# Feed-forward up projections in seven half-size products instead of eight

## The reference

```
y = rms_norm(h, mlp_norm_g[layer])
h = h + square(relu(y @ w_up[layer])) @ w_down[layer]      # w_up 1024 x 4096, w_down 4096 x 1024, f32
```

## Time and profile before

| | |
|---|---|
| runs | 2162.52, 2160.38, 2161.98 us; median 2161.98 |
| profiled execution | span 2157.4 us, its only time in the profile; 4.6 below the median of the runs |
| busy: PE, PEld, DVE, ACT, POOL | 2132.0, 1776.3, 1167.1, 892.1, 966.0 us |
| granted clock of TensorE | 0.997 in the mean |
| two feed-forward stages | from about 1153 to 1490 and 1795 to 2143 us |

### The profile page before, as it was taken

One profiled execution on the slowest core, in us unless ns is written; L12 is line 12 of the kernel. 1 busy time (PEld: TensorE's weight loads), 2 busy tenths in 40 slices (PEclk: granted clock), 3 DMA queues, 4 the chain that ended last, 5 costly groups with the idle time before them and its releaser, 6 DMA issues.

```text
span 2157.4 us, 29579 instructions
## 1 busy us (share of the span) xinstructions
PE 2132.0 (99%) x10318; PEld 1776.3 (82%) x10318; DVE 1167.1 (54%) x1715; ACT 892.1 (41%) x1321; POOL 966.0 (45%) x707
## 2 busy tenths in 40 slices
PE   9999999999999999999999999999999999999998
PEld 7888888778888888878888888888788887888886
DVE  7655556887777777787355222224565565222223
ACT  5433233555655555455534223224345444233223
POOL 4443535355444444316445445444443325444443
PEclk9999999999999999999999999999999999999999
DMA  6232222232222222223222222224212212222221
GB/s 225 87 103 83 97 83 78 89 137 98 79 78 78 84 91 78 104 82 117 98 78 98 98 96 85 98 97 130 98 63 75 79 59 79 98 97 97 97 97 59
DMA packets 38416, 202.09 MB, mean 94 GB/s; under 512 B 4395, under 2 KB 9643, under 8 KB 16076
## 3 DMA queue, kind: packets, MB, share of 16 engines
q1 hardware_dynamic: 29504, 191.46, 25.2%
q10 hardware_dynamic: 8844, 9.70, 1.5%
HBM read 195.90 MB, written 5.24 MB: 93 GB/s over the span
## 4 chain that ended last, share of the span: by engine, by line
PE 89%; DVE 6%; issue 2%; DVEq 2%; ACT 1%; POOL 0%; DMA 0%; POOLq 0%; SPq 0%; ACTq 0%
PE bank L450 15%; PE bank L451 15%; PE bank L456 15%; PE bank L437 12%; PE bank L438 12%; PE bank L439 12%; DVE SS L1799 1%; PE bank L970 1%; PE bank L490 1%; DVE X L2022 1%; PE bank L732 1%; PE bank L491 1%; PE bank L495 1%; DVE T L2019 1%; ACT WH L1126 1%
## 5 line engine op out<-in xcount | busy, mean ns | idle before, releaser
L368 POOL TENSOR_TENSOR WL<-RAW,WH 128x512 fp32r<-128x512 f32 x700 | 959.8, 1402 | 1162.6 <-ACT WH L1126 1162.6
L1126 ACT ACTIVATE WH<-RAW 128x2048 fp32r<-128x2048 f32 (+1 forms) x190 | 337.2, 1777 | 591.3 <-PE bank L439 288.1
L450 PE MATMUL bank<-HH,WH 128*128 128x512 f32 x968 | 382.7, 395 | 0.8 <-DVEq L2353 0.8
L451 PE MATMUL bank<-HL,WH 128*128 128x512 f32 x968 | 377.3, 390 | 0.0
L456 PE MATMUL bank<-HH,WL 128*128 128x512 f32 x968 | 241.5, 391 | 0.0
L450 PEld LDWEIGHTS bank<-HH,WH 128*128 128x128 f32 x968 | 181.8, 188 | 39.9 <-DVEq L2353 1.0
L456 PEld LDWEIGHTS bank<-HH,WL 128*128 128x128 f32 x968 | 181.6, 188 | 39.9 <-issue 2.4
L451 PEld LDWEIGHTS bank<-HL,WH 128*128 128x128 f32 x968 | 181.9, 188 | 37.7 <-issue 1.0
L2319 DVE TENSOR_TENSOR X<-X,bank 128x512 f32<-128x512 f32 x128 | 87.6, 686 | 193.7 <-PE bank L456 117.5
L2310 DVE SCALAR_TENSOR_TENSOR TG<-bank,RS 128x512 f32<-128x512 f32 x64 | 44.0, 688 | 206.9 <-PE bank L439 135.8
L437 PE MATMUL bank<-HH,WH 128*128 128x512 f32 x288 | 112.2, 390 | 0.7 <-DVE HL L1788 0.7
(11 more groups left out here) (440 smaller groups left out, 4364.7 us busy)
## 6 DMA issues: line engine op xcount, KB each, us to landing
RAW<-panels SPq DMA_DIRECT2D x174, 1024.0 KB, 4.8
X<-xin SPq DMA_DIRECT2D x4, 512.0 KB, 7.6
xsave<-X ACTq DMA_DIRECT2D x4, 512.0 KB, 2.8
X<-xsave ACTq DMA_DIRECT2D x1, 2048.0 KB, 13.7
TAB<-scratch ACTq DMA_DIRECT2D x16, 128.0 KB, 3.1
out<-ACC SPq DMA_DIRECT2D x8, 256.0 KB, 2.3
RAW<-panels SPq DMA_DIRECT2D x2, 512.0 KB, 6.6
T<-xtok SPq DMA_DIRECT2D x2, 512.0 KB, 12.7
```

The costliest lines, as they stand in the source:

```text
L368: gp.tensor_tensor(WL[:, s, cs], RAW[:, s, cs], WH[:, s, cs].bitcast(f32), ALU.subtract).then_inc(lo_ready, 1)
L450: nc.tensor.matmul(o, wh[:, columns[k - k0]], xh[:, k, :], start=first and k == k0, stop=False)
L451: nc.tensor.matmul(o, wh[:, columns[k - k0]], xl[:, k, :], start=False, stop=False)
L1126: return nc.scalar.activation(dst, src, ACT.Copy)
```

## The change

Chunk 0 stays as it was (PLAIN = 1). In chunks 1 to 7 an up panel of 256 hidden features is a 2x2 block product: the panel has four blocks (near and far 128 features, upper and lower 512 inputs) and the tokens four (upper and lower 512 inputs, first and last 256 tokens). Instead of eight block products of 12 matmuls (48 of 512 columns in all) it makes seven, of 12 matmuls with 256 columns each, in Winograd's form of Strassen's scheme: products 2 to 4 take sums of weight blocks (SUMS, split into EH and EL) and sums of token blocks (TOK, split into TOKH and TOKL), product 6 a weight block and a sum of tokens, product 7 a sum of weights that stands in the panel itself. The texts call the two halved panels of a chunk H0 and H1; the order on PE is H0, H1, D0, D1.

The sums of tokens are made once for each layer, in chunk 0, behind its hidden tiles: DVE norms all tokens (NORMED), makes four sums, ACT and DVE split sums and normed tokens. DVE makes the weight sums of each halved panel from RAW, writing the last over RAW's fourth block, ahead of ACT's split of that panel. Products 5 and 7 add onto the banks of products 1 and 4. DVE adds the products up from PSUM; ACT copies the first product and the sum of products 1 and 5 out of a bank that is used again. The relu and the square are one DVE operation here. The bias table's DMAs move behind the last hidden part. To make room, buffers share memory, and several semaphores of other stages are merged under one name each with shifted counts (`z_made`, `tanh_made`, `squared`, `mix_prepared`), which is not shown; nor are the parts that chunk 0 and the down panels keep.

```diff
+PLAIN = 1
+HALVES = CHUNKS - PLAIN
+PARTS_SPLIT = 2 + 2 * HALVES
...
+    TOKH = sb("TOKH", [128, 4, 4, 256], f32r, c)
...
+    with ExitStack() as c2:
+        TOK = sb("TOK", [128, 4, 4, 256], f32, c2)
+        NORMED = sb("NORMED", [128, KD, 512], f32, c2)
+    TOKL = sb("TOKL", [128, 4, 4, 256], f32r, c)
+    EH, EL = sb("EH", [128, 2, 3, 512], f32r, c), sb("EL", [128, 2, 3, 512], f32r, c)
...
+        def product(o, a, b, waits=None, onto=False):
+            (ah, al), (bh, bl) = a, b
+            for k in range(4):
+                cs = slice(128 * k, 128 * k + 128)
+                nc.tensor.matmul(o[:, 0:256], ah[:, cs], bh(k), start=k == 0 and not onto, stop=False, skip_group_check=onto)
+                nc.tensor.matmul(o[:, 0:256], ah[:, cs], bl(k), start=False, stop=False, skip_group_check=onto)
+            if waits is not None:
+                low_up_to(*waits)
+            for k in range(4):
+                cs = slice(128 * k, 128 * k + 128)
+                end = nc.tensor.matmul(o[:, 0:256], al[:, cs], bh(k), start=False, stop=k == 3, skip_group_check=onto)
+            return end
+        def halved_panel(i, u):
+            n, s = i * 4 + (n0 + 4 * PLAIN + u), i * 2 + (2 * HALVES * L + u)
+            w = panel(n, (n0 + u) % 2)
+            wh, wl = w[:2]
+            b0 = 4 - 4 * u
+            def block_of_w(j):
+                cs = slice(512 * j, 512 * j + 512)
+                return (wh[:, cs], wl[:, cs])
+            def sum_of_w(j):
+                return EH[:, u, j, :], EL[:, u, j, :]
+            def block_of_h(k0, t0):
+                return (lambda k: HH[:, k0 + k, t0:t0 + 256]), (lambda k: HL[:, k0 + k, t0:t0 + 256])
+            def sum_of_h(j):
+                return (lambda k: TOKH[:, j, k, :]), (lambda k: TOKL[:, j, k, :])
+            made = S["up_product"]
+            pe.wait_ge(S["up_parts_split"], PARTS_SPLIT * L + 2)
+            pe.wait_ge(hi_ready, n + 1)
+            o1 = bank(b0)
+            product(o1, block_of_w(0), block_of_h(0, 0), (w, 0)).then_inc(made, 1)
+            pe.wait_ge(S["up_parts_split"], i * 2 + (PARTS_SPLIT * L + 3 + u))
+            product(bank(b0 + 1), sum_of_w(1), sum_of_h(1)).then_inc(made, 1)
+            product(bank(b0 + 3), sum_of_w(2), sum_of_h(2)).then_inc(made, 1)
+            o3 = bank(b0 + 2)
+            product(o3, sum_of_w(0), sum_of_h(0)).then_inc(made, 1)
+            pe.wait_ge(S["up_copied"], i * 4 + (4 * HALVES * L + 2 * u + 1))
+            product(o1, block_of_w(1), block_of_h(4, 0), (w, 512), True).then_inc(made, 1)
+            product(bank(b0 + 1), block_of_w(2), sum_of_h(3), (w, 1024)).then_inc(made, 1)
+            pe.wait_ge(S["up_fifth_read"], s + 1)
+            product(o3, block_of_w(3), block_of_h(4, 256), (w, 1536), True).then_inc(panel_used, 1)
         first_panel(n0)
         if L == 0:
             sum_of_squares(name)
-        else:
-            other_panels(0, True)
-            first_panel(n0 + 4)
-        with pe.Fori(L, CHUNKS - 1) as c:
-            uses.loop(c, [2] * 4 + [1] * 4, first=L)
-            other_panels(c)
-            first_panel(c * 4 + (n0 + 4))
-        uses.end(CHUNKS - 1 - L)
-        other_panels(CHUNKS - 1)
+        other_panels(0, L == 1)
+        with pe.Fori(0, HALVES) as i:
+            uses.loop(i, [2, 3, 2, 2, 2, 3, 2, 2])
+            halved_panel(i, 0)
+            halved_panel(i, 1)
+            down_panels(i * 4 + (n0 + 4 * PLAIN + 2), i * 4 + (4 * CHUNKS * L + 4 * PLAIN))
+        uses.end(HALVES)
...
+        def high_tokens():
+            act.wait_ge(S["up_parts_f32"], PARTS_SPLIT * L + 2)
+            hi(TOKH[:, :, :, :], TOK[:, :, :, :]).then_inc(S["up_parts_hi"], 1)
+        def high_normed():
+            act.wait_ge(panel_used, n0 + 4 * PLAIN - 2)
+            hi(HH[:, 0:4, 0:256], NORMED[:, 0:4, 0:256])
+            hi(HH[:, 4:8, :], NORMED[:, 4:8, :]).then_inc(S["up_parts_hi"], 1)
+        def high_sums(i, u):
+            act.wait_ge(S["up_parts_f32"], i * 2 + (PARTS_SPLIT * L + 3 + u))
+            hi(EH[:, u, :, :], SUMS[:, :, :]).then_inc(S["up_parts_hi"], 1)
+        def high_of_chunk(i):
+            high_sums(i, 0)
+            split_in(i, 4, n0 + 4 * PLAIN)
+            high_sums(i, 1)
+            split_in(i, 4, n0 + 4 * PLAIN + 1)
+        def halved_chunk(i):
+            s = i * 2 + 2 * HALVES * L
+            for u in range(2):
+                b0 = 4 - 4 * u
+                act.wait_ge(S["up_product"], i * 12 + (12 * HALVES * L + 6 * u + 1))
+                hi(TG[:, u, 0:256], B[b0][:, 0:256]).then_inc(S["up_copied"], 1)
+                act.wait_ge(S["up_product"], i * 12 + (12 * HALVES * L + 6 * u + 5))
+                hi(T[:, 2 * u + 1, 0:256], B[b0][:, 0:256]).then_inc(free[b0], 1)
+                act.drain().then_inc(S["up_copied"], 1)
+                for f in range(2):
+                    if f == 1:
+                        split_in(i, 4, n0 + 4 * PLAIN + 2 + u)
+                    act.wait_ge(S["mlp_relu"], i * 4 + (4 * CHUNKS * L + 4 * PLAIN + 2 * u + f + 1))
+                    hi(HIDH[:, 2 * u + f, :], T[:, 2 * u + f, :]).then_inc(S["mlp_hid_hi"], 1)
+        plain_chunk(0)
+        high_tokens()
+        high_normed()
+        act.drain()
+        high_of_chunk(0)
+        with act.Fori(0, HALVES - 1) as i:
+            halved_chunk(i)
+            high_of_chunk(i + 1)
+        halved_chunk(HALVES - 1)
         if L == 0:
+            act.wait_ge(S["rows_stored"], 64)
+            for kind in range(4):
+                bias_table(kind)
             split_at(n0 + 4 * CHUNKS)
...
+        def normed():
+            for k in range(KD):
+                end = v.scalar_tensor_tensor(NORMED[:, k, :], X[:, k, :], gain(f"mlp{L}", k), RS[:, :], ALU.mult, ALU.mult)
+            end.then_inc(S["up_parts_f32"], 1)
+            ve.drain()
+        def sums_of_tokens():
+            b11, b12, b21, b22 = (NORMED[:, k:k + 4, t:t + 256] for k in (0, 4) for t in (0, 256))
+            v.tensor_tensor(TOK[:, 0], b12, b11, ALU.subtract)
+            v.tensor_tensor(TOK[:, 2], b22, b12, ALU.subtract)
+            ve.drain()
+            v.tensor_tensor(TOK[:, 1], b22, TOK[:, 0], ALU.subtract)
+            ve.drain()
+            v.tensor_tensor(TOK[:, 3], b21, TOK[:, 1], ALU.subtract)
+            ve.drain().then_inc(S["up_parts_f32"], 1)
+        def low_tokens():
+            ve.wait_ge(S["up_parts_hi"], PARTS_SPLIT * L + 1)
+            lo(TOKL[:, :, :, :], TOK[:, :, :, :], TOKH[:, :, :, :]).then_inc(S["up_parts_split"], 1)
+        def low_normed():
+            ve.wait_ge(S["up_parts_hi"], PARTS_SPLIT * L + 2)
+            lo(HL[:, 0:4, 0:256], NORMED[:, 0:4, 0:256], HH[:, 0:4, 0:256])
+            lo(HL[:, 4:8, :], NORMED[:, 4:8, :], HH[:, 4:8, :])
+            ve.drain().then_inc(S["up_parts_split"], 1)
+        def sums_of_w(i, u):
+            slot, first = (n0 + u) % 2, n0 + 4 * PLAIN + u
+            a11, a12, a22, a21 = (RAW[:, slot, 512 * j:512 * j + 512] for j in range(4))
+            ve.drain()
+            ve.wait_ge(raw_loaded[slot], i * 32 + (first // 2 * 16 + 16))
+            v.tensor_tensor(SUMS[:, 2], a11, a21, ALU.subtract)
+            v.tensor_tensor(SUMS[:, 0], a21, a22, ALU.add)
+            ve.drain()
+            v.tensor_tensor(SUMS[:, 1], a22, SUMS[:, 2], ALU.subtract)
+            ve.drain()
+            v.tensor_tensor(a21, a12, SUMS[:, 1], ALU.subtract)
+            ve.drain().then_inc(S["up_parts_f32"], 1)
+        def low_sums(i, u):
+            ve.wait_ge(S["up_parts_hi"], i * 2 + (PARTS_SPLIT * L + 3 + u))
+            lo(EL[:, u, :, :], SUMS[:, :, :], EH[:, u, :, :]).then_inc(S["up_parts_split"], 1)
+        def halved_up(i, u):
+            b0 = 4 - 4 * u
+            made, ahead = S["up_product"], 12 * HALVES * L + 6 * u
+            first, second, third = TG[:, u, 0:256], TG[:, u, 256:512], R[:, 256 * u:256 * u + 256]
+            near, far = T[:, 2 * u, :], T[:, 2 * u + 1, :]
+            ve.wait_ge(S["up_copied"], i * 4 + (4 * HALVES * L + 2 * u + 1))
+            ve.wait_ge(made, i * 12 + (ahead + 2))
+            v.tensor_tensor(second, B[b0 + 1][:, 0:256], first, ALU.add).then_inc(free[b0 + 1], 1)
+            ve.drain()
+            ve.wait_ge(made, i * 12 + (ahead + 3))
+            v.tensor_tensor(third, B[b0 + 3][:, 0:256], second, ALU.add).then_inc(free[b0 + 3], 1)
+            ve.drain()
+            ve.wait_ge(made, i * 12 + (ahead + 4))
+            v.tensor_tensor(near[:, 256:512], B[b0 + 2][:, 0:256], third, ALU.add).then_inc(S["up_fifth_read"], 1)
+            ve.wait_ge(made, i * 12 + (ahead + 6))
+            v.tensor_tensor(near[:, 0:256], B[b0 + 1][:, 0:256], third, ALU.add).then_inc(free[b0 + 1], 1)
+            ve.drain()
+            v.scalar_tensor_tensor(near, near, 0.0, near, ALU.max, ALU.mult).then_inc(S["mlp_relu"], 1)
+            ve.wait_ge(panel_used, i * 4 + (n0 + 4 * PLAIN + u + 1))
```

(106 more changed lines are left out.)

72 lines of the change are left out of this document (30 added, 42 removed).

## The result

The changed kernel takes 2177.4 us (median of 4 runs, 2176.07 to 2179.1). Beside it the kernel before took 2162.0, so the ratio is 1.0074, with an interval of [1.0062, 1.0086]: slower by 15.4 us.

What follows compares the result with a forecast made beforehand. It took PE, the matmul engine, as the bound: 13.4 + 16.3 us of waits + 2 x 3.5 for a late product 5 - 23.4 of gain = +13.3 us, from 2161.98 to 2175.3 us; range 2165 to 2188.

Steps and rivals of the forecast that it cites:

- late product 5: In each layer's first H0, product 5 waits for ACT's copy of product 1: 3.5 us a layer.
- The gain: On PE, halved up panels take 10.05 us instead of 10.88: 0.83 us a panel, 23.4 us over both layers.
- faster rival: On PE, products stream closer than 0.1196 us a matmul; at 0.1067 the kernel takes 2145 us; chance 0.04 of faster.
- The chain: Serial DVE and ACT work from chunk 0's last hidden low part to H0's start: 31.0 us (27.9 to 33.6).
- PE's waits: PE idle before chunk 1's first product: 13.4 us in layer 0, 16.3 us in layer 1.
- The clock: Half clock in H0's first products after the idle: 1.7 us a layer, hidden by the copy wait, counted as nothing.
- early product 5: Case in H0 where product 5 is not late: by the skill's rule 1.7 us a layer on top, 3.4 in all.
- The loop: Later halved chunks run without a stall, at 41.9 us each.
- the uncovered loop: Rival: ACT's copy of product 1 comes 3 us later in 14 chunks, +11 us, 2187; chance 0.13.
- The cheap chain: Rival: chain near its lower bound in both layers and product 5 early, 0 to +4, 2162 to 2166; chance 0.08.
- The sum on the median: Whole kernel: +13.3 us, made on the profiled span of 2157.4, put on the median 2161.98: 2175.3 us.

Runs made afterwards that it cites:

- Norming twice: The changed kernel with DVE's norming of the tokens of chunk 0 done twice over, 8 more operations a layer: 2187.8 us, 1.0126 of before.
- keeping PE busy: Weight sums first, plus PE multiplying unused tiles (56 and 68 in the two layers) between chunk 0's down projections and the first halved panel: 2178.4 us (one run).
- copy first: Weight sums first, plus ACT copying the first product ahead of the second halved panel's split, in every halved chunk: 2175.8 us (one run).
- both edits: Weight sums first, plus PE kept busy with unused multiplications and ACT's copy of the first product ahead of the second panel's split: 2174.9 us (one run).
- all three orders: The changed kernel, one plain chunk, with weight sums first, copy first, and DVE's first additions ahead of the second panel's low sums: 2170.2 us, 1.0041 of before.
- the fastest: Two plain chunks instead of the changed kernel's one, copy first, and DVE's first three additions ahead of the second panel's low sums: 2146.0 us, 0.9926 of before.
- weight sums first: The changed kernel with DVE's sums of the first halved panel's weights ahead of the down projections' additions and the low parts: 2176.0 us, 1.0065 of before.

## Why the prediction was right

The forecast was 2175.3 us and the time is 2177.4: PE idle behind the chain, plus a late product 5, less a small gain a panel. The forecast was short by 1.3 us in the gain, 0.4 in the waits and 0.4 in product 5, which add up to the 2.1, so the total is not right by errors that cancel. By its steps:

- **The gain**: 22.1 us instead of 23.4. A panel of products takes 10.08 us, as forecast; the saving is 0.79 a panel and not 0.83, because the step weighed a spacing of 0.1196 against 0.2267, and in the changed kernel it is 0.120. The formula of the Trainium skill (TensorE: Matmul & The Clock Gate, section "Back-to-back issue gap"), 109 ns here, is not what these rows show; the section gives it for the gap of a single isolated matmul, and the prediction used it for a stream. Nor do they show the faster rival's spacing, and its argument was too strong: 4 of a product's 12 matmuls use the weights of the one before, a third and not half.
- **The chain**: 31.5 us from the last low part's end (1178.03) to H0's start, forecast 31.0. The norming was mis-sized: 8.49 us, where the prediction had 7.6 and an upper bound of 7.8. The bound took POOL's split as it was before, over 3.6 us after the norming began. But the norming holds POOL up in turn: POOL's four parts for D1's panel (1176.19 to 1182.58) now take 6.39 us instead of 5.48 and end 4.6 us after the norming began. Three of the eight operations fall beside POOL instead of 2.3, and they start 1.70 us apart (1177.95, 1179.65, 1181.35, 1183.05), near the 1.6 of the prediction; the other five start 0.66 apart. Norming twice shows the price by itself, 8.49 beside POOL and 5.39 without it. The other terms with the handovers came out 0.4 us shorter together (most of it the weight sums, 2.90 from 1203.18 to 1206.08 against 3.2), so that by luck nearly half of the norming's error does not show in the chain.
- **PE's waits**: 13.71 and 16.42 us, forecast 13.4 and 16.3.
- **The late product 5**: 3.71 us a layer, forecast 3.5; the copy, not the clock, ended it. The runs show more than the prediction claimed: the half clock, the copy and DVE's first addition stand behind one another, the copy 1.60 us behind the half clock in layer 0 and the addition 0.69 behind that once the copy is first, so that none could be mended alone.
- **The clock**: counted at nothing, and keeping PE busy showed that it was covered where it stood. Its place moves, though: behind the copy waits of 1.72, 2.50, 2.52, 2.94 and 3.28 us in the experiments the clock was down, and behind those of 0.58 to 1.60 us it was not. For the Trainium skill's rule on idle gaps (the same page, section "HAM oscillation — how this bites in real kernels") these runs agree that a gap in a burst of matmuls can cost clock behind it, and they show it already at gaps shorter than the waits in that section's example. The 3.4 us that I worked out by it for an early product 5 did not come. With the copy first, product 5 starts 8.08 and 7.92 us after H0's start instead of 9.38, without a wait; yet taking the half clock away there (both edits) leaves the distances at 59.08 and 61.82 instead of 59.06 and 61.48, since the addition is late as well.
- **The loop**: 41.94 us a chunk without a wait, forecast 41.9, so the rival of the uncovered loop is out. The bias table's DMAs moved and cost PE nothing.
- **The cheap chain**: not the changed kernel's, with 13.71 and 16.42 us. With all three orders the waits come down to 10.33 and 12.66, which is this rival's 10.2 and 13.2; but the rival also needed an early product 5, and there H0 still runs 4.1 us late in each layer (24.25 and 24.27 us from its start to D0, against 2 x 10.08). Two slips in the working change nothing: the upper bounds of the chain add up to 33.3 with the handovers and not 33.6, and five terms, not six, are without slack.
- **The sum on the median**: it was made on one profiled span. The profiled spans differ by 18.5 us, the medians by 15.4. In the runs that have both numbers on record, the time is 2.1 us above the span; so the profiled execution of the kernel before would have taken about 2159.5, which is 2.5 below its median, and that of the changed kernel, 2177.98, is 0.6 above its own. The last section says where the other 3 us lie.

## What to carry to other kernels

A change that saves on the busiest engine at the price of a serial start on the others has to be priced at the start first: here 22 us of saving against 30 us of idle time, with one plain chunk to hide a chain that needs more than its down projections. Give the chain a stage long enough to lie beside: one more plain chunk costs 3.2 us of saving, and with it the kernel goes from 15.4 us slower than before to 12.2 faster. And look for what is late next: of three things that end together, one taken away gives little, three reorderings together gave 6.9 us.

## What the runs showed of the hardware

The granted clock did not fall at the same waits in every run. Before the second feed-forward stage PE waits 1.5 us for the norm's sums, both before and after the change. In the profiled run before, the matmuls behind that wait took 2.84 us to the next line (1807.09 to 1809.93), in the changed kernel's 4.42 (1813.39 to 1817.81), eight matmuls of 512 columns at half clock. The rows, the changed kernel first, then the kernel before:

```profile
1813.39 1.21 PE L520 MATMUL bank<-ONES,SUMS 128*128 128x2 f32 x8 [1.48 <-DVEq L1899]
1814.46 3.52 PE L470 MATMUL bank<-HH,WL 128*128 128x512 f32 x8
```

```profile
1807.09 1.05 PE L506 MATMUL bank<-ONES,SS 128*128 128x2 f32 x8 [1.49 <-DVEq L1801]
1808.00 2.09 PE L456 MATMUL bank<-HH,WL 128*128 128x512 f32 x8
```

The same happened at the end of the kernel, where both wait 2.44 us and the changed kernel's matmuls then took 1.87 instead of 1.05 us and 3.75 instead of 2.91. Together these are the 3 us by which the profiled spans differ more than the medians. The runs of one kernel lie up to 5.4 us apart (2142.6 to 2148.0 in the fastest). That this is the clock at such waits fits the traces. The stage ahead of the second feed-forward is the same in the kernel before and in those with one or four plain chunks, and PE waits 1.48 to 1.50 us there in each; half clock followed in the profiled runs of the changed kernel, weight sums first, copy first and all three orders, and did not in those of the kernel before, norming twice, four plain chunks, PE kept busy and both edits. The 27 runs of the kernel before beside the experiments agree: those with a mean granted clock of 0.998 took 2160.4 us in the mean, those with 0.996 took 2162.3. But only one run of each kernel has a trace, so for the scatter as a whole it is not shown.

The three kernels with two plain chunks wait 2.51 us there instead of 1.48, and half clock followed in each; so 1.0 us of what they lack of the 19 us, and the half clock behind it, stand outside the halved chunks.
